# A gated recurrence carried between 128-token chunks by chained states, in a three-layer block on one core

## The reference, cut to what matters

```python
def hgrn2_chunked(q, k, v, log_f):
    """S_t = diag(f_t) S_{t-1} + k_t v_t^T, o_t = S_t^T q_t, with k_t = 1 - f_t."""
    ...
    G = jnp.cumsum(log_f, axis=3)
    q_dec = q * jnp.exp(G)
    k_inv = k * jnp.exp(-G)
    k_to_end = k * jnp.exp(G_last - G)
    scores = jnp.where(causal, jnp.einsum('nbhtd,nbhsd->nbhts', q_dec, k_inv), 0.0)
    o_intra = jnp.einsum('nbhts,nbhsv->nbhtv', scores, v)
    def step(state, xs):
        q_c, k_c, v_c, decay_c = xs
        o_inter = jnp.einsum('bhtd,bhdv->bhtv', q_c, state)
        new_state = decay_c^T * state + jnp.einsum('bhsd,bhsv->bhdv', k_c, v_c)
        return new_state, o_inter
```

## Time and profile before

| | us |
|---|---|
| three runs | 1465.63, 1467.60, 1467.93 (median 1467.6) |
| the profiled execution | 1465.37, its span 1463.5 |
| PE busy | 1430.4 (98%) |
| DVE busy | 955.3 (65%) |
| ACT busy | 860.6 (59%) |
| POOL busy | 63.6 (4%) |
| ACT idle in front of the exponential L1445, rounds 3 to 7 | 1.40 each |
| mean granted TensorE clock | 0.995 |

### The profile page before, as it was taken

The page is one execution under the profiler, slowest core; times in us unless marked ns, Lnnn a source line. Parts: engine busy times, 40 slices in busy tenths (PEclk is TensorE's granted clock), DMA queues, the critical chain, the costliest instruction groups (busy, mean ns, idle before and its releaser), DMA issues.

```text
span 1463.5 us, 24784 instructions
## 1 busy us (share of the span) xinstructions
PE 1430.4 (98%) x10076; PEld 924.8 (63%) x10076; DVE 955.3 (65%) x1926; ACT 860.6 (59%) x1241; POOL 63.6 (4%) x149
## 2 busy tenths in 40 slices
PE   7999999999999999999999999999999999899998
PEld 4444477556568548576688864746695855366677
DVE  6732556888679675555677524578667337799974
ACT  6554456777564665454563654457655466678863
POOL 0000000000000000000010000100100000000000
PEclk9999999999999999999999999999999999999999
DMA  6323223213332433433232332330223433100002
GB/s 195 107 95 113 88 87 97 76 59 115 100 102 87 136 113 98 141 112 113 95 108 67 113 110 87 96 108 1 61 87 116 144 110 98 58 2 2 2 3 100
DMA packets 128497, 131.85 MB, mean 90 GB/s; under 512 B 9896, under 2 KB 125392, under 8 KB 128256
## 3 DMA queue, kind: packets, MB, share of 16 engines
q1 hardware_dynamic: 126096, 121.62, 26.0%
q0 software_dynamic: 2288, 8.64, 1.7%
HBM read 128.12 MB, written 2.10 MB: 89 GB/s over the span
## 4 chain that ended last, share of the span: by engine, by line
PE 82%; DVE 13%; ACT 2%; issue 1%; DMA 1%; SPq 0%; DVEq 0%; POOL 0%; ACTq 0%
PE bank L739 14%; PE bank L741 14%; PE bank L740 14%; PE bank L782 8%; PE bank L783 8%; PE bank L784 8%; DVE tmin L2525 4%; DVE scr L2543 2%; DVE bank L2521 2%; PE bank L908 1%; PE bank L926 1%; DVE wring L1976 1%; PE bank L1063 1%; PE bank L1158 1%; PE bank L862 1%
## 5 line engine op out<-in xcount | busy, mean ns | idle before, releaser
L739 PE MATMUL bank<-xT,whigh 128*128 128x512 f16 x952 | 361.1, 379 | 0.3 <-DVE wring L1976 0.2
L741 PE MATMUL bank<-xT,wring 128*128 128x512 f16 x952 | 361.1, 379 | 0.0
L740 PE MATMUL bank<-xT,whigh 128*128 128x512 f16 x952 | 361.1, 379 | 0.0
L1976 DVE SCALAR_TENSOR_TENSOR wring<-wring,wsc,whigh 128x2048 f16<-128x2048 f32 (+2 forms) x106 | 245.2, 2313 | 137.1 <-ACT whigh L1347 136.5
L1347 ACT ACTIVATE whigh<-wring,wsc 128x2048 f16<-128x2048 f32 (+2 forms) x106 | 209.0, 1972 | 109.5 <-DVE wsc L1879 90.4
L1364 ACT ACTIVATE whigh<-wring 128x2048 bf16<-128x2048 f32 (+2 forms) x106 | 199.1, 1878 | 92.1 <-DMA wring<-in_w_down 31.2
L782 PE MATMUL bank<-whigh,slab 128*128 128x256 f16 x800 | 218.1, 273 | 1.8 <-DVE wring L1976 1.3
L783 PE MATMUL bank<-wring,slab 128*128 128x256 f16 x800 | 218.1, 273 | 0.0
L784 PE MATMUL bank<-whigh,slab 128*128 128x256 f16 x800 | 218.1, 273 | 0.0
L739 PEld LDWEIGHTS bank<-xT,whigh 128*128 128x128 f16 x952 | 93.2, 98 | 112.8 <-issue 2.7
L741 PEld LDWEIGHTS bank<-xT,wring 128*128 128x128 f16 x952 | 93.0, 98 | 112.5
(11 more groups left out here) (335 smaller groups left out, 2270.2 us busy)
## 6 DMA issues: line engine op xcount, KB each, us to landing
wring<-in_w_in SPq DMA_DIRECT2D x27, 1024.0 KB, 5.1
wring<-in_w_up SPq DMA_DIRECT2D x16, 1024.0 KB, 5.4
wring<-in_w_down SPq DMA_DIRECT2D x16, 1024.0 KB, 5.4
wring<-in_even_w_in SPq DMA_DIRECT2D x14, 1024.0 KB, 5.4
wring<-in_odd_w_in SPq DMA_DIRECT2D x14, 1024.0 KB, 5.1
wring<-in_w_a SPq DMA_DIRECT2D x4, 1024.0 KB, 5.4
wring<-in_w_out SPq DMA_DIRECT2D x4, 1024.0 KB, 5.4
wring<-in_even_w_out SPq DMA_DIRECT2D x4, 1024.0 KB, 5.1
```

The source lines that it names most:

```text
L739: pe.matmul(bank, wh[:, k, wcol:wcol + width], xh[:, k, :], start=k == 0, stop=False)
L740: pe.matmul(bank, wh[:, k, wcol:wcol + width], xl[:, k, :], start=False, stop=False)
L741: mm = pe.matmul(bank, wl[:, k, wcol:wcol + width], xh[:, k, :], start=False, stop=k == KC - 1)
L1976: dve.scalar_tensor_tensor(low_of(i)[:, :, 0:m], loaded(i)[:, :, 0:m], wsc[:, n:n + 1], high_of(i)[:, :, 0:m], ALU.mult, ALU.subtract).the ...
```

## The change

Only the products inside the four blocks stay products of scores. What one block leaves to the next goes through a state of 128 x 128 for each head:

- PE: in `hgrn_scores` the products across blocks give way to three transposes of K[3]. A new `hgrn_sums(h-1)` stands between the two tiles of round h: three products of turned keys and values, one for each of the first three blocks. `hgrn_pv` is four products of 128 tokens (before: 512, 384, 256, 128) and, behind a wait for `hg_st`, three products of a state with Q[3].
- ACT: three copies of `hgrn_copies` fall away. `hgrn_turned(h-1)`, one copy of 128 x 384, stands right behind the logarithm of head h. In round 8 the gates come ahead of the copies.
- DVE: the fourth level (two operations of 128 x 256) and its two small copies fall away. `hgrn_states(h-1)`, a copy and two multiply-adds of 128 x 128 that read PSUM, each waiting for the one before, stands between `hgrn_levels(h)` and `measure`.
- POOL's four DMAs into `side` wait for `hg_pv` 7 instead of `hg_lvl` 35, since Q[3] is now read by `hgrn_pv`.
- The forget logits are 96 matmuls of 8 columns by 128 tokens. The four token groups go to four banks and to four quarters of the partitions (0, 32, 64, 96). ACT reads them with four operations, and the bias is loaded four times, once for each quarter.

```diff
--- before.py
+++ after.py
...
+        def turned_keys(h, c):
+            return prob[:, 4 * (h % 2), (c + 1) * P:(c + 2) * P]
+
+        def state(h, c):
+            return prob[:, 4 * (h % 2) + 3, (c - 1) * P:c * P]
+
+        def chunk_decay(h):
+            return (segdec, mulq)[h % 2][:, 3, 0:TT]
...
                 if n == split_index("wa", 0):
-                    pool.wait_ge(s_("hg_lvl"), 5 * (HEADS_H - 1))
+                    pool.wait_ge(s_("hg_pv"), HEADS_H - 1)
                     for t in range(TT):
...
+            def forget_tile(w):
+
+                (wh, wl), (xh, xl) = w, xhalves
+                for k in range(KC):
+                    for n, (ww, xx) in enumerate(((wh, xh), (wh, xl), (wl, xh))):
+                        for t in range(TT):
+                            mm = pe.matmul(SA[t][32 * t:32 * t + 8, 0:P], ww[:, k, 0:8], xx[:, k, t * P:(t + 1) * P],
+                                           start=k == 0 and n == 0, stop=k == KC - 1 and n == 2)
+                mm.then_inc(s_("fl_mm"), 1)
...
             def hgrn_scores(h):
...
-                    elif i == 3:
-
-                        pe.matmul(bank[:, 0:P], K[3][:, 0:P], Q[3][:, P:2 * P], start=True, stop=True)
-                        pe.matmul(bank[:, P:3 * P], K[4][:, 0:P], Q[4][:, 2 * P:4 * P], start=True, stop=True)
-                        mm = pe.matmul(bank[:, 3 * P:4 * P], K[3][:, 2 * P:3 * P], Q[3][:, 3 * P:4 * P],
-                                       start=True, stop=True)
                     else:
-                        mm = pe.matmul(bank[:, 0:2 * P], K[4][:, P:2 * P], Q[4][:, 2 * P:4 * P], start=True, stop=True)
+                        for j in range(TT - 1):
+                            mm = pe.transpose(bank[:, j * P:(j + 1) * P], K[3][:, j * P:(j + 1) * P], ident[:, :])
                     mm.then_inc(s_("hg_lvl"), 1)
+
+            def hgrn_sums(h):
+
+                bank = score_bank(h, 4)
+                pe.wait_ge(s_("hg_eva"), 2 * h + 1)
+                for c in range(TT - 1):
+                    mm = pe.matmul(bank[:, c * P:(c + 1) * P], turned_keys(h, c), vtok[:, c, h * P:(h + 1) * P], start=True, stop=True)
+                mm.then_inc(s_("hg_lvl"), 1)
 
             def hgrn_pv(h):
...
                 for j in range(TT):
-                    mm = pe.matmul(SB[0][:, j * P:], vtok[:, j, h * P:(h + 1) * P],
-                                   prob[:, 4 * (h % 2) + j, j * P:], start=j == 0, stop=j == TT - 1)
+                    pe.matmul(SB[0][:, j * P:(j + 1) * P], vtok[:, j, h * P:(h + 1) * P],
+                              prob[:, 4 * (h % 2) + j, j * P:(j + 1) * P], start=j == 0, stop=False, skip_group_check=True)
+                pe.wait_ge(s_("hg_st"), h + 1)
+                for j in range(1, TT):
+                    mm = pe.matmul(SB[0][:, j * P:(j + 1) * P], state(h, j), side[:, 9 * (h % 2) + 7, j * P:(j + 1) * P],
+                                   start=False, stop=j == TT - 1, skip_group_check=True)
                 mm.then_inc(s_("hg_pv"), 1)
...
-                for key in (("ga", "og"), ("og", "ga"))[h % 2]:
+                for at, key in enumerate((("ga", "og"), ("og", "ga"))[h % 2]):
+                    if at == 1 and h >= 1:
+                        hgrn_sums(h - 1)
...
-            feat_tile("fl", w, 0, xhalves, SA[0][0:8, :], width=8)
+            forget_tile(w)
...
                 if h < HEADS_H:
                     gate_logs(h)
+                if 1 <= h <= HEADS_H:
+                    hgrn_turned(h - 1)
                 if h >= 2:
...
-                act.wait_ge(s_("hg_lvl"), r + 2)
-                bank = SA[(r + 1) % 4]
-                act.activation(prob[:, p0, P:4 * P], bank[:, 0:3 * P], ACT.Copy)
-                act.activation(prob[:, p0 + 2, 3 * P:4 * P], bank[:, 3 * P:4 * P], ACT.Copy).then_inc(s_("hg_eva"), 1)
-                act.wait_ge(s_("hg_eva"), own(s_("hg_eva")))
-                act.wait_ge(s_("hg_lvl"), r + 3)
-                act.activation(prob[:, p0 + 1, 2 * P:4 * P], SA[(r + 2) % 4][:, 0:2 * P], ACT.Copy).then_inc(s_("hg_eva"), 1)
+
+            def hgrn_turned(h):
+
+                act.wait_ge(s_("hg_lvl"), 5 * h + 4)
+                if h >= 2:
+                    act.wait_ge(s_("hg_pv"), h - 1)
+                act.activation(prob[:, 4 * (h % 2), P:4 * P], SA[(5 * h + 3) % 4][:, 0:3 * P], ACT.Copy).then_inc(s_("hg_eva"), 1)
...
             for h in range(HEADS_H + 2):
+                if h >= 1:
+                    hgrn_gates(h)
                 if h == HEADS_H:
                     hgrn_copies(h - 1)
-                if h >= 1:
-                    hgrn_gates(h)
...
-            ins = act.activation(frow[0], SA[0][0:8, :], ACT.Identity, bias=bf_[:, 0:1], scale=undo("fl", 0)[0:8, :])
+            for t in range(TT):
+                r = slice(32 * t, 32 * t + 8)
+                ins = act.activation(frow[0][:, t * P:(t + 1) * P], SA[t][r, 0:P], ACT.Identity, bias=bf_[r, 0:1], scale=undo("fl", 0)[r, :])
...
                 if h >= 2:
-                    dve.wait_ge(s_("hg_lvl"), 5 * (h - 1))
+                    dve.wait_ge(s_("hg_pv"), h - 1)
...
-                for l in range(1, 4):
+                for l in (1, 2):
                     n, w = 32 >> l, CH << l
                     dve.wait_ge(dve_chain, joined)
-                    if l < 3:
-                        joins(l + 1)
+                    if l == 1:
+                        joins(2)
                         joined = own(dve_chain)
...
-
-                        dve.tensor_tensor(by(Q[4], 4)[:, 2:4, :], by(Q[3], 4)[:, 2:4, :], wide(mulq[:, 3, 2:4], 2, w), ALU.mult)
-                        ins = dve.tensor_tensor(by(K[4], 4)[:, 0:2, :], by(K[3], 4)[:, 0:2, :], wide(mulk[:, 3, 0:2], 2, w), ALU.mult)
...
+            def hgrn_states(h):
+
+                dve.wait_ge(s_("hg_lvl"), 5 * h + 5)
+                sums = SA[(5 * h + 4) % 4]
+                dve.tensor_copy(state(h, 1), sums[:, 0:P]).then_inc(dve_chain, 1)
+                dve.wait_ge(dve_chain, own(dve_chain))
+                dve.scalar_tensor_tensor(state(h, 2), state(h, 1), chunk_decay(h)[:, 1:2], sums[:, P:2 * P], ALU.mult, ALU.add).then_inc(dve_chain, 1)
+                dve.wait_ge(dve_chain, own(dve_chain))
+                dve.scalar_tensor_tensor(state(h, 3), state(h, 2), chunk_decay(h)[:, 2:3], sums[:, 2 * P:3 * P], ALU.mult, ALU.add).then_inc(s_("hg_st"), 1)
...
                 if 1 <= h < HEADS_H:
                     hgrn_levels(h)
+                if 1 <= h <= HEADS_H:
+                    hgrn_states(h - 1)
                 if 1 <= h <= HEADS_H:
                     measure(first_og + h + 1)
```

More of the change, by code:

```diff
@@ L163, in build @@
         gng = sb("gng", [P, 4])
-        bf_ = sb("bf_", [8, 1])
+        bf_ = sb("bf_", [P, 1])
         bgate = sb("bgate", [P, 48])
@@ L386, in build @@
             (gng[:, :], a["even_gn_g_2"][0].rearrange("(k p) -> p k", p=P)),
-            (bf_[:, :], a["even_b_f_2"][0].rearrange("(k p) -> k p", p=1)),
+            *((bf_[32 * t:32 * t + 8, :], a["even_b_f_2"][0].rearrange("(k p) -> k p", p=1)) for t in range(TT)),
             (bgate[:, :], a["odd_b_gate_2"].to_broadcast([P, 48])),
@@ L888, in tok_and_norm, with score_bank @@
                 projected(0, w0, parts[2])
+            def score_bank(h, i):
+                r = 5 * h + i
+                if r >= 4:
+                    h0, i0 = divmod(r - 4, 5)
+                    if i0 < 2:
+                        pe.wait_ge(s_("hg_evd"), 2 * h0 + i0 + 1)
+                    elif i0 < 4:
+                        pe.wait_ge(s_("hg_eva"), 2 * h0 + 4 - i0)
+                    else:
+                        pe.wait_ge(s_("hg_st"), h0 + 1)
+                return SA[r % 4]
             def hgrn_scores(h):
                 b = h % 2
[L893 to L905, removed]
+                K = [kT[:, h, :]] + [side[:, 9 * b + 1 + i, :] for i in range(3)]
+                Q = [qT[:, h, :]] + [side[:, 9 * b + 5 + i, :] for i in range(3)]
+                for i in range(4):
+                    bank = score_bank(h, i)
+                    pe.wait_ge(s_("hg_lv"), 4 * h + i + 1)
                     if i < 3:
@@ L1191, in _ @@
             pe.wait_ge(s_("hg_evd"), 16)
-            pe.wait_ge(s_("hg_eva"), 24)
+            pe.wait_ge(s_("hg_eva"), 16)
             pe.wait_ge(s_("gated"), 6)
@@ L2241, in hgrn_levels @@
                 b = h % 2
-                K = [kT[:, h, :]] + [side[:, 9 * b + 1 + i, :] for i in range(4)]
-                Q = [qT[:, h, :]] + [side[:, 9 * b + 5 + i, :] for i in range(4)]
+                K = [kT[:, h, :]] + [side[:, 9 * b + 1 + i, :] for i in range(3)]
+                Q = [qT[:, h, :]] + [side[:, 9 * b + 5 + i, :] for i in range(3)]
                 def by(x, n):
@@ L2257, in joins @@
                     dve.tensor_copy(mq[:, :, 1], seg[:, :, 0])
-                    if l < 3:
-                        dve.tensor_tensor(segdec[:, l + 1, 0:n // 2], seg[:, :, 0], seg[:, :, 1], ALU.mult)
```

(5 more changed lines are left out.)

12 lines of the change are left out of this document (4 added, 8 removed).

## The result

| | median of runs, us | profiled execution, us (span) | ratio to before, 95% |
|---|---|---|---|
| before | 1467.1 (1465.6 to 1467.9) | 1465.4 (1463.5) | |
| after | 1479.3 (1475.9 to 1483.4) | 1477.7 (1475.9) | 1.0088 (1.0072 to 1.0104) |

A forecast was written before the change was run, and what follows sets the result against it. PE and a DVE and ACT ring of waits were taken as almost level bounds. Recurrence + 6.7 and forget logits - 2.7 gave + 4.0 us: 1469.4 against the profiled 1465.4, 1471.6 on the median, stated as 1471, range 1463.5 to 1475.

The forecast's parts named there:

- the turned copy is hidden: ACT's `hgrn_turned`, 0.5 us, falls into 1.40 us of ACT idle before its exponentials; without that cover, 0.5 a round.
- PE's idle of about 2 us a round: Sign in the profile: PE idle about 1.9 us a round before the first state product, ended by the third state operation.
- the ring's 18.4 us a round: Chain of waits through DVE, PE and ACT each round: 6.6 + 3.84 + 7.98 = 18.4 us, against PE's 17.4 before.
- PE's answer to the states: From the end of the state operations (S): square at S + 1.1, scores from S + 0.9, scan at S + 6.6.
- S(2): S is when a head's state operations on DVE end and its states are ready; for head 2 forecast at 296.4.
- the two small copies that I credited: Copies removed at the end of DVE's levels, 311.64 to 311.78, counted as 0.14 us less a round.
- POOL's step: POOL's DMAs wait for `hgrn_pv(6)` and delay the first `wa` slot's all-reduce: `high` there at 375.2 instead of 371.8.
- the fourth rival of the prediction: POOL does not matter; sums behind the last `ga` tile decide: + 2.5 in all, 1468 to 1470 us, chance 0.08.
- The forget logits: On PE, 24 matmuls in 5.2 us become 96 at 0.025 each, 2.4 us: 2.7 saved, bounds 0 and 3.9.
- savings arrive: Rival: PE's savings arrive in full, 8 x 0.9 + 2.7 = 9.9 us less, 1456 to 1458, chance 0.12.
- Ring unchanged: Rival: the recurrence's chain of waits stays at 17.66 us a round; + 0.9 in all, 1466 to 1469, chance 0.18.
- quarters do not overlap: Rival: the forget logits' four column quarters do not work at once; + 6.7 alone, 1472 to 1474.5, chance 0.12.

The follow-up runs named there:

- the wait filled: Changed kernel with eight idle f16 matmuls of 512 tokens, output never read, in front of PE's wait for the states: 1473.9 us, ratio 1.0049.
- POOL's loads later: Changed kernel with POOL's four loads of x one step later, behind the all-reduce of the first wa slot: 1478.2 us, ratio 1.0077.
- the first four experiments: Forget logits alone on the kernel before, 1462.7; changed kernel with old forget logits, 1482.4; with POOL's loads one step later, 1478.2; with idle matmuls in PE's wait, 1473.9 us.
- The new order: Changed kernel with states in front of the output of head h-2, behind it in the last round, POOL's loads one step later: 1458.2 us, ratio 0.9944.

## Why the prediction was wrong

Right were the direction, the mechanism (`hg_st` pulls the square and the scores into the ring), that the turned copy is hidden, that a transpose is one pass (three in 0.33 us, 301.02 to 301.35), and PE's idle of about 2 us a round.

- **The step that failed is the ring's 18.4 us a round**, in its term for PE's answer to the states. It came from rows at full clock and gave the square at S + 1.1, the first mask at S + 2.0 and the scan at S + 6.6. In the changed kernel they come at S + 1.8, 3.5 and 8.1; with the wait filled at S + 1.1 (318.37), 2.0 and 6.6, as forecast. I had written down 1.9 us of idle PE in each round and did not ask what that does to the clock. At the lower clock the same passes take nearly twice as long, and the round is 20.3.
- **Where the 8.45 us lie by which the recurrence was mis-sized.** S(2), the S of head 2, comes at 297.51 instead of 296.4: 1.1. From there S(6) takes 80.4 us instead of 4 x 18.4 = 73.6; with the wait filled it takes 75.6, so 4.8 are the clock and 2.0 the terms below. Round 8, S(6) to S(7), takes 14.0 instead of 13.3: 0.7, in which POOL's step has a part.
- **Smaller terms of the same ring.** S came 8.67 after L2368 (307.92 to 316.59) in round 4, 8.33 in the next two and 8.68 in round 7, not 7.98. The states' two multiply-adds, whose factor is a column of 128 values, take 0.35 each, where the operation of the earlier trace rows, with a constant as its factor, gave 0.28, and start 0.38 apart. The second full product of the levels waits for its own predecessor (0.78 apart instead of 0.60); before, the two small copies that I credited stood in that place, so the credit is nothing. In round 4 there is 0.35 more between L2368 and L2372 (1.20 instead of 0.85), whose cause the profile does not show. With full clock all this made rounds of 18.7 to 19.1.
- **POOL's step**: the place and the 3.2 us were right, the price was not. Of the 3.25 us 0.6 were on the path, because the sums behind the last tile come nearly as late. That the sums decide is the fourth rival of the prediction, which I had at 0.08 and for another reason (an all-reduce that is not held up). The 1.5 us by which the forecast lies above that rival should be 0.6.
- **The forget logits**: 3.8 saved instead of 2.7. The floor of 0.025 a matmul from the earlier trace rows does not hold here: 96 in 1.34 us are 0.014 each, a quarter of 0.054. The bound of 3.9 was the truth. The Trainium skill (TensorEngine Tiling (Array Packing)) has both rules. By its Theoretical Speedup, up to 4x at 32 columns, the estimate for the stage was 1.3 us, and the trace's 1.34 agrees. Its Instruction Overhead, on which I had settled, does not show in these matmuls on four different quarters.
- **Not foreseen at all**: 2.0 us at the load of `w_out`. The transfer, not the order, differs: ACT waits 2.73 to 2.75 us in the profiles of before, of before with the new forget logits and of the filled wait, 4.71 in that of after, and 3.8 to 4.8 in all the others. Why is open; it was not tested.

The change's own runs spread over 7.5 us (before: 2.3). Their mean clocks are 0.989 to 0.994, the slowest run having the lowest and the fastest the highest, while with the wait filled they are 0.995 to 0.996 and the spread 4.3. This fits a fall of the clock in more or fewer rounds: in the profiled run it falls in all of rounds 4 to 7, in that with POOL's loads later not in round 5. It is no proof, for before itself spreads over 6.7 us in the 16 runs beside the first four experiments, its two slowest with the lowest clock too (0.993).

The rivals: "savings arrive" failed by the place of three small operations, and came true when they were moved: rounds of 16.78 us against PE's 16.5. "Ring unchanged" and "quarters do not overlap" are out.

## What to carry to other kernels

When an engine's product comes to be waited for in mid-round, list everything queued behind the waiting instruction, and price the wait of PE twice: as time, and as slower passes behind it, since rows at full clock may not hold there. Put the small operations that release such a wait where their engine is idle in front of a wait of its own, and check the last round apart, since what comes late there is another thing. The new order, with POOL's loads one step later, gained 21 us without one instruction less.

## What the runs showed of the hardware

- Four groups of 32 columns of the array, each with 8 used, work on four matmuls at once without a visible floor: 96 f16 matmuls of 128 tokens in 1.34 to 1.45 us.
- PE's clock in this stage: in the changed kernel the passes behind waits of 1.20, 1.51 and 1.93 us ran at full speed, and behind waits of 2.35, 2.02, 2.00 and 2.36 at the lower level at first. The length of the wait alone does not decide: behind one of 2.35 (317.11, POOL's loads later) six passes ran at full speed before the clock fell, and behind the same wait of 1.9 in the same kernel it stayed up in one trace (372.37) and fell in another (371.80). Eight idle matmuls in the wait kept the level up and took 5.5 us off four rounds.
- A 128 x 128 multiply-add on DVE that reads PSUM takes 0.35 us with a column of 128 values as its factor, 0.28 with a constant; it is 0.38 us from one to a dependent next. The two also read and write different tiles, so that the factor is the reason is not shown.
